# Three dense stages of a decoder kernel divided into parts, with gathered expert rows served between the parts

## The chip, the cores and the metric

The kernel runs on one core of a Trainium2 chip. The core has engines that run their own instruction streams and meet through semaphores: TensorE (PE, matmuls and transposes into PSUM), VectorE (DVE), ScalarE (ACT), GpSimd (POOL) and SyncE (SP), and 16 DMA engines. The metric is the device time of one execution in microseconds. The kernel before took 3770.63 us as the median of three runs, which lie between 3755.8 and 3774.13.

## The reference

Two layers over 512 tokens of width 1024. Each layer computes three branches from one projection of the normed input, adds them through gates, then adds a mixture over 16384 single-neuron experts (PEER), then a small gated embedding.

```python
h = _rms(x, g_mix)
z = h @ w_in                       # diff q,k,v | mla latents | conv B,C,value | 3 gates
y_d = _diff_attention(dq, dk, dv, ...)          # 4 heads of 2 x 64, QK-norm, ALiBi
y_m = _mla(cq, ckv, kr, g_cq, w_uq, g_ckv, w_ukv, g_q, g_k)
y_c = _short_conv(cb, cc, cx, conv_w)
mixed = g0 * (y_d @ w_br_diff) + g1 * (y_m @ w_br_mla) + g2 * (y_c @ w_br_conv)
x = x + mixed @ w_out
x = x + _peer(_rms(x, g_ffn), w_query, sub_keys, u_experts, v_experts)
x = x + sigmoid(_rms(x, g_ple) @ w_ple_gate) * (p_i @ w_ple_proj)

# inside _mla
q  = (_rms(c_q, g_cq) @ w_uq)      # 512 x 256 @ 256 x 768, 8 heads of 96
kv = (_rms(c_kv, g_ckv) @ w_ukv)   # 512 x 128 @ 128 x 1024, 8 heads of 64 (k) + 64 (v)
# q and k: RMSNorm over the 96 of a head, then RoPE on the last 32, then causal attention

# inside _peer, for each token: 8 heads choose 16 experts each, 128 rows of two tables
act = gelu(einsum('thkd,td->thk', u_tab[expert], hc))
out = einsum('thk,thkd->td', gate * act, v_tab[expert])
```

## The kernel before, in words

All data is f32. The tokens are worked in halves of 256 of one layer; a half is called d, from 0 to 3 (d = 0 and 1 are layer 0, d = 2 and 3 layer 1), and consists of two token tiles of 128. The program goes in steps from -1 to 4. In step s the dense stages of half s + 1 run (projections, both attentions, convolution, gates, output, and the choice of the experts), and beside them the expert rows of half s.

An *expert row* is, for the 128 tokens of a token tile, one chosen expert per token: one indirect DMA by POOL brings 128 x 2048 floats (1 MB: a row of u and a row of v) into one of 8 slots of `ring`. A half has 256 such rows (128 per token tile). DVE multiplies the u part with the token and sums (line 1173, a *dot*); ACT takes the gelu (line 750) and multiplies with the gate (line 752, the *weight*). Then the v part is added in one of two ways, fixed ahead by `BY_PE`: either DVE multiplies with the weight and adds to x (line 1182), or ACT makes a diagonal matrix of the weights (line 758, four of them in turn) and PE adds diag times v in `ps_sum` (line 1299, two matmuls of 512 columns, which the profile records as four). POOL may issue the gather of row n only when row n - 8 is added, so a slot that PE or DVE does not finish holds back all later gathers.

The order is a plan that all engines follow. `stages_of(step)` lists the stages, and `ROWS_IN` says how many expert rows go in front of each; `timeline()` turns this into a whole number of rows. On each engine the program then is `serve(rows)`, stage, `serve(rows)`, stage. For DVE and ACT `serve` does the rows at once. PE keeps the rows of a stage in a list `fresh` and does them behind the stage, when the next stage's `serve` comes, unless a slot or a diagonal is needed sooner: for most stages the next `serve` does them before that stage's own matmuls; for stages in `ROWS_LAST` (the scores among them) behind the stage. In step -1 and step 4 no rows are served.

PSUM has three banks that PE fills for ACT (`ps_act`) and three for DVE (`ps_dve`), each used in turn: PE may begin the fourth when the first is emptied (an evacuation, line 523 on ACT).

The stages that the change touches, for each half:
- `diff_turn`: after the q and k of the differential attention are normed on DVE, PE transposes them (line 1345), 4 heads x (q, k) = 8 banks of 256 columns, and ACT empties each into `diff_qT` or the key cache, with a gain.
- `mla_up`, called *up* here: PE multiplies the normed latents with `w_uq` (line 1495) and `w_ukv` (line 1498): per token tile four banks, which ACT empties in six activations (the two banks of k and v in two pieces each). Then DVE sums the squares for the norms (`mla_sums`, line 951 first), norms and turns.
- `mla_turn`, called *mla's turn*: PE transposes the finished q and k of 8 heads, 16 banks, ACT empties each (96 x 256). The scores of the first head (line 1430, 1432) wait for the last of them. DVE takes the scores (line 1020), ACT takes the exponential (line 537).

## Time and profile before

| | |
|---|---|
| median of three runs | 3770.63 us (3755.8 to 3774.13) |
| profiled execution, its own time | 3764.78 us |
| its span | 3762.9 us |
| mean granted PE clock | 0.893 of full |
| busy share PE, DVE, ACT, POOL | 78%, 66%, 40%, 35% |
| bytes moved by DMA | 1298.53 MB, mean 345 GB/s |
| gathers of expert rows | 1024, median 11.8 us from issue to landing |

The profile is one execution. In its rows a time in square brackets is how long the engine sat idle before the group, with the engine that released it. Matmuls in f32 appear as two records each, so one expert row on PE is x4. PEclk is the clock that was granted to PE as a share of full speed. The gathers begin at about 490 us, and from about 3120 us on only the last expert rows run, beside nothing dense; between them lie steps 0, 1 and 2.

### The profile page before, as it was taken

The numbers are of one execution on the slowest core, as the hardware profiler recorded it, in microseconds if no ns is written. First come the engines' busy times: TensorE is split into PE (matmuls) and PEld (weight loads), VectorE is DVE, ScalarE is ACT, GpSimd is POOL, SyncE is SP. The second block draws the span as 40 slices with busy tenths as digits, with TensorE's granted clock in tenths as the row PEclk, the third lists the DMA queues.
The fourth block names the chain that finished last, engine by engine and source line by source line (L and its number), as shares of the span: only waits on it lengthen the run. The fifth ranks groups of instructions, "written<-read, shape, count | busy, mean of one in ns | idle before, by whom it ended". The sixth has DMA issues, their size and how long they took to land.

```text
span 3762.9 us, 28794 instructions
## 1 busy us (share of the span) xinstructions
PE 2923.3 (78%) x8144; PEld 1489.6 (40%) x8144; DVE 2488.2 (66%) x5163; ACT 1486.5 (40%) x3998; POOL 1333.3 (35%) x1033
## 2 busy tenths in 40 slices
PE   7699858767988788767989788867998785555556
PEld 4454624534436334433436234524446331111112
DVE  1311487775667876876658877766657877777774
ACT  2230234467433344457432344458433342222222
POOL 0000043333332443344333443334333445555551
PEclk9889979988999899989999899889999997777778
DMA  4214379989998999989998999989999999999994
GB/s 151 81 67 162 121 319 384 378 337 343 393 385 348 394 402 386 395 351 407 405 377 322 409 410 381 357 340 361 382 389 360 390 405 419 422 422 422 422 421 185
DMA packets 182399, 1298.53 MB, mean 345 GB/s; under 512 B 20320, under 2 KB 21856, under 8 KB 26592
## 3 DMA queue, kind: packets, MB, share of 16 engines
q0 software_dynamic: 147456, 1073.81, 70.7%
q1 hardware_dynamic: 34784, 222.88, 15.1%
q8 instruction: 66, 1.08, 0.1%
q14 instruction: 93, 0.76, 0.1%
HBM read 1294.51 MB, written 2.10 MB: 345 GB/s over the span
## 4 chain that ended last, share of the span: by engine, by line
PE 47%; DMA 20%; DVE 14%; ACT 13%; issue 5%; POOL 1%; SPq 0%; DVEq 0%; ACTq 0%; POOLq 0%
DMA ring<-in_uv,experts 17%; PE ps_sum L1299 12%; PE ps_act L1361 8%; PE ps_act L1533 8%; PE ps_act L1406 7%; DVE ring L1173 5%; DMA wt<-in_weights 4%; PE ps_dve L1361 3%; DVE x L1182 2%; PE ps_dve L1561 2%; ACT L750 2%; ACT L537 2%; ACT diag L758 2%; ACT weight L752 2%; ACT area_e L537 2%
## 5 line engine op out<-in xcount | busy, mean ns | idle before, releaser
L507 POOL DMA_INDIRECT ring<-in_uv,experts x1024 | 1330.8, 1300 | 2358.3 <-DVE x L1182 915.6
L1299 PE MATMUL ps_sum<-ring,diag 128*128 128x512 f32 x2120 | 1228.6, 723 | 660.1 <-ACT diag L758 654.1
L1173 DVE SCALAR_TENSOR_TENSOR ring<-ring,h_ffn 128x1024 f32<-128x1024 f32 x1024 | 1233.4, 1219 | 207.3 <-DMA ring<-in_uv,experts 201.2
L1299 PEld LDWEIGHTS ps_sum<-ring,diag 128*128 128x128 f32 x2120 | 440.1, 222 | 1328.9 <-ACT diag L758 921.6
L1182 DVE SCALAR_TENSOR_TENSOR x<-ring,weight,x 128x1024 f32<-128x1024 f32 x494 | 633.0, 1281 | 220.0 <-ACT weight L752 219.9
L750 ACT ACTIVATE dots<-dots 128x1 f32<-128x1 f32 x1024 | 205.5, 201 | 1350.7 <-DVE ring L1173 1348.2
L1406 PE MATMUL ps_act<-area_h,wt 128*128 128x256 f32 x1536 | 345.1, 383 | 2.6 <-ACT area_h L523 2.6
L1533 PE MATMUL ps_act<-wt,area_h 128*128 128x512 f32 x768 | 339.5, 597 | 9.2 <-DMA wt<-in_weights 9.1
L1361 PE MATMUL ps_act<-wt,area_h 128*128 128x512 f32 (+1 forms) x768 | 332.5, 593 | 5.1 <-ACT area_h L523 5.1
L1406 PEld LDWEIGHTS ps_act<-area_h,wt 128*128 128x128 f32 x1536 | 293.1, 192 | 58.1 <-issue 15.3
L752 ACT ACTIVATE weight<-dots,gate 128x1 f32<-128x1 f32 x1024 | 301.6, 295 | 33.3
L1533 PEld LDWEIGHTS ps_act<-wt,area_h 128*128 128x128 f32 x768 | 145.2, 191 | 197.3 <-issue 177.1
L1361 PEld LDWEIGHTS ps_act<-wt,area_h 128*128 128x128 f32 x768 | 149.3, 196 | 182.9 <-issue 175.0
L523 ACT ACTIVATE area_b<-ps_act 128x256 f32<-128x256 f32 (+1 forms) x208 | 87.8, 437 | 335.0 <-PE ps_act L1406 143.7
L758 ACT ACTIVATE diag<-ident,weight 128x128 f32<-128x128 f32 x530 | 212.9, 402 | 17.4
L750 ACT ACT_TABLE_LOAD x143 | 183.5, 1283 | 2.5
L1561 PE MATMUL ps_dve<-wt,area_t 128*128 128x512 f32 x384 | 168.7, 592 | 0.0
L1345 PE MATMUL ps_act<-ident,area_b 128*128 128x128 f32 (+1 forms) x448 | 84.9, 336 | 87.2 <-DVE area_b L815 41.7
L537 ACT ACT_TABLE_LOAD x107 | 137.3, 1283 | 1.9
L1034 DVE TENSOR_TENSOR area_b<-ps_dve,area_b 128x512 f32<-128x512 f32 x32 | 22.1, 691 | 150.3 <-PE ps_dve L1561 150.3
L1020 DVE CUSTOM_DVE_ANT_0 area_e<-ps_dve,mask 128x128 f32<-128x128 f32 (+3 forms) x64 | 31.2, 489 | 124.1 <-PE ps_dve L1432 67.6
L1361 PE MATMUL ps_dve<-wt,area_b 128*128 128x512 f32 x256 | 110.9, 594 | 1.9 <-ACT area_b L523 1.9
(171 smaller groups left out, 2107.1 us busy)
## 6 DMA issues: line engine op xcount, KB each, us to landing
wt<-in_weights SPq DMA_DIRECT2D x192, 1024.0 KB, 8.9
ring<-in_uv,experts POOLq DMA_INDIRECT x1024, 11.8
wt<-in_weights SPq DMA_DIRECT2D x12, 512.0 KB, 8.9
wt<-in_weights SPq DMA_DIRECT2D x4, 768.0 KB, 8.9
x<-in_x SPq DMA_DIRECT2D x4, 512.0 KB, 5.2
area_y<-in_keys SPq DMA_DIRECT2D x4, 512.0 KB, 9.8
area_f<-in_keys SPq DMA_DIRECT2D x4, 512.0 KB, 11.2
area_f<-in_ffn_rows SPq DMA_DIRECT2D x4, 512.0 KB, 4.5
```

The lines of the kernel that those rows point to most:

```text
L507: pool.indirect_dma_start(ring[:, row.slot, :], None, a[f"uv{row.step // 2}"][:, :], bass.IndirectOffsetOnAxis(ap=experts[:, row.step % 2, ...
L537: act.activation(*args, **kw).then_inc(act_ops, 1)
L750: act.activation(dots[:, j], dots[:, j], ACT.Gelu).then_inc(gelu_ready, 1)
L752: act.activation(weight[:, j], dots[:, j], ACT.Copy, scale=gate[:, row.step % 2, row.tile, j])\
L758: act.activation(diag[:, row.pe_before % DIAGS, :], ident[:, :], ACT.Copy, scale=weight[:, j])\
L1173: dve.scalar_tensor_tensor(u, u, 1.0, h_ffn[:, row.tile, :], ALU.mult, ALU.mult, accum_out=dots[:, row.j:row.j + 1]).then_inc(dots_ready, 1)
L1182: dve.scalar_tensor_tensor(xs, ring[:, row.slot, D:2 * D], weight[:, row.j:row.j + 1], xs, ALU.mult, ALU.add)\
L1299: ins = pe.matmul(ps_sum[:, b, :], diag[:, row.pe_before % DIAGS, :], ring[:, row.slot, D + b * 512:D + (b + 1) * 512], start=row.pe_first ...
L1361: ins = pe.matmul(banks[t][:, 0:width], lhsT[:, 4 * kh + k, t * P:(t + 1) * P], w[:, k, 0:width], start=(kh + k == 0), stop=(kh == 1 and k ...
L1406: ins = pe.matmul(b[:, 0:HALF], w[:, k, c * P:(c + 1) * P], hT[:, k, :], start=(k == 0), stop=(k == KT - 1))
L1533: ins = pe.matmul(bank, hT[:, 4 * kh + k, t * P:(t + 1) * P], w[:, k, :], start=(kh + k == 0), stop=(kh == 1 and k == 3))
L1561: ins = pe.matmul(b, (ydT, ymT, ycT)[br][:, k, t * P:(t + 1) * P], w[:, k, :], start=(k == 0), stop=(k == 3))
```

## The change

Three stages are listed in parts. `diff_turn` becomes two stages of two heads each, `mla_up` two stages of one token tile each, `mla_turn` four stages of two heads each. The number of rows in front of them is divided in the same way (1.5 into 2 x 0.75, 5 into 2 x 2.5, 4 into 4 x 1). The scores wait for the last part. The weight tiles of up are released after its second part, as before.

```diff
-    "diff_sq": (0, 0, 0, 2), "diff_norm": (0, 1, 0, 3), "diff_turn": (8, 0, 0, 0),
+    "diff_sq": (0, 0, 0, 2), "diff_norm": (0, 1, 0, 3), "diff_turn": (4, 0, 0, 0),
-    "mla_norm": (3, 5, 0, 5), "mla_up": (8, 4, 0, 0), ... "mla_turn": (16, 0, 0, 0),
+    "mla_norm": (3, 5, 0, 5), "mla_up": (4, 2, 0, 0), ... "mla_turn": (4, 0, 0, 0),
 ROWS_IN = {
-    ... "diff_turn": 1.5, ... "mla_up": 5, ... "mla_turn": 4, ...
+    ... "diff_turn": 0.75, ... "mla_up": 2.5, ... "mla_turn": 1, ...
@@ stages_of
-        out += [..., ("qkv", d, 2), ("diff_turn", d)]
+        out += [..., ("qkv", d, 2), ("diff_turn", d, 0), ("diff_turn", d, 1)]
-        out += [("mla_norm", d), ("mla_up", d), ("mla_sums", d), ("mla_qk", d), ("mla_rope", d), ("mla_turn", d)]
+        out += [("mla_norm", d), ("mla_up", d, 0), ("mla_up", d, 1), ("mla_sums", d), ("mla_qk", d), ("mla_rope", d)]
+        out += [("mla_turn", d, part) for part in range(4)]
@@ ACT
-            def diff_turn(at, d):
-                for h in range(DH):
+            def diff_turn(at, d, part):
+                for h in range(2 * part, 2 * part + 2):
-            def mla_up(at, d):
-                for t in range(2):
+            def mla_up(at, d, t):
-            def mla_turn(at, d):
-                for h in range(MH):
+            def mla_turn(at, d, part):
+                for h in range(2 * part, 2 * part + 2):
@@ PE
-                pe.wait_ge(evacs, WHERE[("diff_turn", d)].evacs + 8)
+                pe.wait_ge(evacs, WHERE[("diff_turn", d, 1)].evacs + 4)
-            def mla_up(at, d):
-                pe.wait_ge(evacs, at.evacs)
+            def mla_up(at, d, t):
+                if t == 0:
+                    pe.wait_ge(evacs, at.evacs)
...
-                release(2)
+                if t:
+                    release(2)
-                pe.wait_ge(evacs, WHERE[("mla_turn", d)].evacs + 16)
+                pe.wait_ge(evacs, WHERE[("mla_turn", d, 3)].evacs + 4)
```

The plan gives these rows in front of the stages: up 4, 5, 5 rows at d = 1, 2, 3, now 2 + 2, 3 + 2, 3 + 2; mla's turn 4 each, now 1 + 1 + 1 + 1; diff's turn 2 each, now 1 + 1. Which rows go by PE is unchanged, and so is the order on DVE.

On PE at d = 1, from the first matmul of up to the second head's scores, before (L1495 and L1498 are up, L1299 expert rows at two matmuls each, L1345 with 96x128 mla's turn, L1430 and L1432 the scores):

```order
L1495 MATMUL ps_act<-wt,area_f 128x512 x2
L1495 MATMUL ps_act<-wt,area_f 128x256 x2
L1498 MATMUL ps_act<-wt,area_f 128x512 x2
L1299 MATMUL ps_sum<-ring,diag 128x512 x20
L1345 MATMUL ps_act<-ident,area_b 96x128 x32
L1430 MATMUL ps_dve<-kept_mla_kT,area_b 128x256
L1432 MATMUL ps_dve<-area_kv,area_b 128x128
L1299 MATMUL ps_sum<-ring,diag 128x512 x6
```

And in the changed kernel, at the same place:

```order
L1299 MATMUL ps_sum<-ring,diag 128x512 x4
L1495 MATMUL ps_act<-wt,area_f 128x512 x2
L1495 MATMUL ps_act<-wt,area_f 128x256 x2
L1498 MATMUL ps_act<-wt,area_f 128x512 x2
L1299 MATMUL ps_sum<-ring,diag 128x512 x16
L1345 MATMUL ps_act<-ident,area_b 96x128 x8
L1299 MATMUL ps_sum<-ring,diag 128x512 x2
L1345 MATMUL ps_act<-ident,area_b 96x128 x8
L1299 MATMUL ps_sum<-ring,diag 128x512 x2
L1345 MATMUL ps_act<-ident,area_b 96x128 x16
L1430 MATMUL ps_dve<-kept_mla_kT,area_b 128x256
L1299 MATMUL ps_sum<-ring,diag 128x512 x2
```

The first half of up stands ahead of the first row shown. Two rows (x4) moved from behind up to between its halves, and two of the three rows that stood behind the first scores now stand between quarters of the turn, one each. At d = 3 the quarters hold rows at other places (16 transposes, a row, 8, a row, 8), and none stands behind the first scores.

On ACT at d = 3, from the diag of up's third expert row on, before (L523 is the evacuation, L750 gelu, L752 weight, L758 diag):

```order
L758 ACTIVATE diag<-ident,weight 128x128
L750 ACTIVATE dots<-dots 128x1
L752 ACTIVATE weight<-dots,gate 128x1
L758 ACTIVATE diag<-ident,weight 128x128
L750 ACTIVATE dots<-dots 128x1
L752 ACTIVATE weight<-dots,gate 128x1
L523 ACTIVATE area_b<-ps_act 128x512
L523 ACTIVATE area_b<-ps_act 128x256
L523 ACTIVATE area_b<-ps_act 128x4x64
L523 ACTIVATE area_kv<-ps_act 128x256
```

And in the changed kernel (where the evacuation's line is L524):

```order
L758 ACTIVATE diag<-ident,weight 128x128
L524 ACTIVATE area_b<-ps_act 128x512
L524 ACTIVATE area_b<-ps_act 128x256
L524 ACTIVATE area_b<-ps_act 128x4x64
L524 ACTIVATE area_kv<-ps_act 128x256
L524 ACTIVATE area_b<-ps_act 128x4x64
L524 ACTIVATE area_kv<-ps_act 128x256
L750 ACTIVATE dots<-dots 128x1
L752 ACTIVATE weight<-dots,gate 128x1
L758 ACTIVATE diag<-ident,weight 128x128
L750 ACTIVATE dots<-dots 128x1
L752 ACTIVATE weight<-dots,gate 128x1
```

The fourth and fifth expert row of up moved from ahead of its first evacuation to behind its sixth activation, between the two token tiles.

## Rows read from the trace of the kernel before

**Rows 1.** The page: its span, and busy us of the engines.
```profile
span 3762.9 us, 28794 instructions
...
PE 2923.3 (78%) x8144; PEld 1489.6 (40%) x8144; DVE 2488.2 (66%) x5163; ACT 1486.5 (40%) x3998; POOL 1333.3 (35%) x1033
```

**Rows 2.** Waits in 500:3000 (DVE) and 2470:2535 (POOL): total us, times, longest.
```profile
DVE ring L1173 <- DMA ring<-in_uv,experts: 39.8, 37, 12.1
...
POOL ring L507 <- PE ps_sum L1299: 31.0, 4, 16.1
```

**Rows 3.** Timeline, POOL and DVE, up at d = 3: start, us, what [idle before].
```profile
2486.22 0.94 POOL L507 DMA_INDIRECT ring<-in_uv,experts  x1 [16.07 <-PE ps_sum L1299]
...
2494.48 1.22 DVE L1173 SCALAR_TENSOR_TENSOR ring<-ring,h_ffn 128x1024 f32<-128x1024 f32 x1 [12.13 <-DMA ring<-in_uv,experts]
...
2496.82 1.75 DVE L951 TENSOR_TENSOR area_e<-area_b 128x1536 f32<-128x1536 f32 x1
```

**Rows 4.** Timeline, PE, up at d = 3.
```profile
2471.47 4.54 PE L1495 MATMUL ps_act<-wt,area_f 128*128 128x512 f32 x8 [0.86 <-ACT area_f L523]
...
2478.81 1.13 PE L1498 MATMUL ps_act<-wt,area_f 128*128 128x512 f32 x2 [1.94 <-ACT area_b L523]
2479.78 2.74 PE L1495 MATMUL ps_act<-wt,area_f 128*128 128x512 f32 x8
...
2484.07 8.75 PE L1299 MATMUL ps_sum<-ring,diag 128*128 128x512 f32 x20
```

**Rows 5.** Timeline, ACT, up at d = 3.
```profile
2474.56 0.40 ACT L758 ACTIVATE diag<-ident,weight 128x128 f32<-128x128 f32 x1
...
2478.18 1.12 ACT L523 ACTIVATE area_b<-ps_act 128x512 f32<-128x512 f32 x3
...
2486.76 0.29 ACT L752 ACTIVATE weight<-dots,gate 128x1 f32<-128x1 f32 x1
```

**Rows 6.** Timeline, DVE, up at d = 1.
```profile
785.22 1.28 DVE L1182 SCALAR_TENSOR_TENSOR x<-ring,weight,x 128x1024 f32<-128x1024 f32 x1 [4.32 <-ACT weight L752]
...
796.18 1.23 DVE L1173 SCALAR_TENSOR_TENSOR ring<-ring,h_ffn 128x1024 f32<-128x1024 f32 x1 [0.62 <-DMA ring<-in_uv,experts]
```

**Rows 7.** Timeline, DVE and PE, up at d = 2.
```profile
1634.61 1.28 DVE L1182 SCALAR_TENSOR_TENSOR x<-ring,weight,x 128x1024 f32<-128x1024 f32 x1 [5.71 <-ACT weight L752]
...
1625.80 2.07 PE L1498 MATMUL ps_act<-wt,area_f 128*128 128x512 f32 x2 [4.37 <-ACT area_b L523]
```

**Rows 8.** Timeline, ACT, PE and POOL, mla's turn at d = 1.
```profile
822.98 0.46 ACT L523 ACTIVATE area_b<-ps_act,mq_gain 96x256 f32<-96x256 f32 x1
...
828.86 0.48 ACT L523 ACTIVATE area_kv<-ps_act,cols 96x256 f32<-96x256 f32 x1
...
836.87 0.62 ACT L537 ACTIVATE area_e<-area_e,soft 128x384 f32<-128x384 f32 x1 [1.51 <-DVE soft L1020]
...
823.49 5.25 PE L1345 MATMUL ps_act<-ident,area_b 128*96 128x128 f32 x26 [6.28 <-ACT area_b L523]
...
830.16 5.32 PE L1299 MATMUL ps_sum<-ring,diag 128*128 128x512 f32 x12
...
832.31 0.94 POOL L507 DMA_INDIRECT ring<-in_uv,experts  x1 [11.72 <-PE ps_sum L1299]
```

**Rows 9.** Timeline, ACT, second exponential at d = 2 and d = 3.
```profile
1684.76 0.40 ACT L537 ACTIVATE area_e<-area_e,soft 128x128 f32<-128x128 f32 x1 [0.60 <-DVE soft L1020]
...
2542.57 0.62 ACT L537 ACTIVATE area_e<-area_e,soft 128x384 f32<-128x384 f32 x1
```

**Rows 10.** Windows over expert rows on PE: us, PE busy, PEclk, DMA share, GB/s.
```profile
627.20:630.90 3.70, 3.70 (x7) 0.50 0.88 363
783.10:793.40 10.30, 10.30 (x25) 1.00 0.88 352
```

**Rows 11.** Timeline, PE, rows behind diff's first scores, d = 2 and 3.
```profile
1479.80 3.78 PE L1299 MATMUL ps_sum<-ring,diag 128*128 128x512 f32 x4
...
2321.25 5.52 PE L1299 MATMUL ps_sum<-ring,diag 128*128 128x512 f32 x8
```

More of the change, by code:

```diff
@@ L127, in tiles_done @@
     if name == "mla_up":
-        return [("for_act", at.evacs + 8)] * 2
+        return [("for_act", at.evacs + 4)] * 2
     if name in ("conv_x", "branch_first", "branch_more"):
@@ L176, in stages_of @@
     if d < STEPS:
-        out += [("x_norm", d), ("qkv", d, 0), ("qkv", d, 1), ("diff_sq", d), ("diff_norm", d), ("qkv", d, 2), ("diff_turn", d)]
+        out += [("x_norm", d), ("qkv", d, 0), ("qkv", d, 1), ("diff_sq", d), ("diff_norm", d), ("qkv", d, 2), ("diff_turn", d, 0), ("diff_turn", d, 1)]
         out += attention("diff", d, DH, [("conv_c", d, 0), ("conv_c", d, 1), ("conv_x", d, 0), ("conv_x", d, 1),
@@ L212, in timeline @@
             base = [a + b for a, b in zip(base, counts(st))]
-            tiles = TILES_OF.get(st[0], 0)
+            tiles = TILES_OF.get(st[0], 0) if st[0] != "mla_up" or st[2] else 0
             if tiles:
@@ L647, in mla_norm @@
                 evac(ckvT, bank(HALF), scale=col("g_ckv", d // 2))
-            def mla_up(at, d):
-                for t in range(2):
-                    row = qm[:, t, :, :].rearrange("p h d -> p (h d)")
-                    evac(row[:, 0:512], bank())
-                    evac(row[:, 512:768], bank(256))
-                    for i in range(2):
-                        part = bank().rearrange("p (h d) -> p h d", h=4)
-                        evac(km[:, t, 4 * i:4 * i + 4, 0:MNOPE], part[:, :, 0:MNOPE], last=False)
-                        evac(mla_v[d % 2][:, t, 256 * i:256 * (i + 1)].rearrange("p (h d) -> p h d", h=4),
-                             part[:, :, MNOPE:MNOPE + MV])
+            def mla_up(at, d, t):
+                row = qm[:, t, :, :].rearrange("p h d -> p (h d)")
+                evac(row[:, 0:512], bank())
+                evac(row[:, 512:768], bank(256))
+                for i in range(2):
+                    part = bank().rearrange("p (h d) -> p h d", h=4)
+                    evac(km[:, t, 4 * i:4 * i + 4, 0:MNOPE], part[:, :, 0:MNOPE], last=False)
+                    evac(mla_v[d % 2][:, t, 256 * i:256 * (i + 1)].rearrange("p (h d) -> p h d", h=4),
+                         part[:, :, MNOPE:MNOPE + MV])
             def mla_qk(at, d):
@@ L1419, in nothing, with diff_turn @@
                 pass
-            def diff_turn(at, d):
+            def diff_turn(at, d, part):
                 pe.wait_ge(dve_ops, at.dve)
-                for h in range(DH):
+                for h in range(2 * part, 2 * part + 2):
                     for c in range(2):
@@ L1484, in mla_norm, with mla_turn @@
                     turn_tiles(lambda t: latent[:, t, k * P:(k + 1) * P])
-            def mla_up(at, d):
-                pe.wait_ge(evacs, at.evacs)
+            def mla_up(at, d, t):
+                if t == 0:
+                    pe.wait_ge(evacs, at.evacs)
                 uq = tile(0)[:, 0:1536].rearrange("p (k n) -> p k n", k=2)
                 ukv = tile(1)
-                for t in range(2):
-                    ts = slice(t * P, (t + 1) * P)
-                    for lo, hi in ((0, 512), (512, 768)):
-                        b = act_bank()
-                        for k in range(2):
-                            ins = pe.matmul(b[:, 0:hi - lo], cqT[:, k, ts], uq[:, k, lo:hi], start=(k == 0), stop=(k == 1))
-                        to_act(ins)
-                    for i in range(2):
-                        to_act(pe.matmul(act_bank(), ckvT[:, ts], ukv[:, 512 * i:512 * (i + 1)], start=True, stop=True))
-                release(2)
-            def mla_turn(at, d):
+                ts = slice(t * P, (t + 1) * P)
+                for lo, hi in ((0, 512), (512, 768)):
+                    b = act_bank()
+                    for k in range(2):
+                        ins = pe.matmul(b[:, 0:hi - lo], cqT[:, k, ts], uq[:, k, lo:hi], start=(k == 0), stop=(k == 1))
+                    to_act(ins)
+                for i in range(2):
+                    to_act(pe.matmul(act_bank(), ckvT[:, ts], ukv[:, 512 * i:512 * (i + 1)], start=True, stop=True))
+                if t:
+                    release(2)
+            def mla_turn(at, d, part):
                 pe.wait_ge(dve_ops, at.dve)
-                for h in range(MH):
+                for h in range(2 * part, 2 * part + 2):
                     for source in (qm, km):
```

6 lines of the change are left out of this document (3 added, 3 removed).

## The prediction

> **What bounds the kernel now.** I read the page first. Its busy shares [rows 1] name no engine at its limit: PE is busy 78% of the span and DVE 66%. Then I asked who waits for whom. Between 500 and 3000 us, where the expert rows run beside the dense layers, DVE waits for a gather 37 times and 39.8 us in all [rows 2], of 2500. So up to there it is not the transfers but the hand-over between PE, ACT and DVE that sets the pace. After that the last 240 rows stream alone, and nothing of the change lies there. The program works on four halves of 256 tokens (d = 0 to 3). For d = 0 no expert row runs beside the dense stages, so splitting a stage there puts nothing between its parts: cost 0. That leaves nine places: diff's turn, up and mla's turn, each at d = 1, 2 and 3. I looked at each in the timeline, engine by engine, and asked what ends last.
>
> One place stands out, up at d = 3. Of the 39.8 us above, 12.1 are one wait: POOL waited 16.07 us for PE to be done with a slot of the ring, issued the gather at 2486.22, and DVE got it at 2494.48 [rows 2, 3]. PE was busy with up from 2471.47 and came to the expert rows only at 2484.07, four records a row, 8.75 us for 20 records or 1.75 us a row [rows 4]. In the middle of up PE also waited 1.94 us for ACT, which served five expert rows first and began to empty banks at 2478.18 [rows 4, 5].
>
> **The change, part by part.** No arithmetic is added, and on DVE the order is what it was. The expert rows that stood ahead of a stage on ACT, or behind it on PE, now stand partly between its parts. So there is no new instruction to pay, only what each engine has in front of it. On PE, up gets two rows between its halves at each d, mla's turn two single rows between its quarters at each d, and diff's turn one row at d = 2 and d = 3 and none at d = 1. On ACT the gelu, weight and diag of the same rows are spread likewise.
>
> *Up at d = 3.* ACT serves three rows, the third done at 2474.96 [rows 5], and then empties the first bank, not at 2478.18. PE's fourth bank starts at about 2476.7 and the first half ends at about 2477.8 (the matmul of that bank now takes 1.13 us [rows 4]). The first expert row is done 1.75 us later, at 2479.5, and POOL issues at about 2480.0, 6.2 us sooner. The same transfer of 8.3 us (2486.22 to 2494.48) lands at 2488.3, and the sums, which now start 2.3 us behind it at 2496.82 [rows 3], start at 2490.6: -6.2. Another path could be later. PE's second half starts behind two rows, at 2481.3, takes 4.3 us as now (2479.78 to 2484.07 [rows 4]) and ends at 2485.6, 1.5 us later than now; the weight that DVE needs ahead of the sums comes at 2487.05 now, 3.0 us after PE's end [rows 5], then at 2488.6, and the sums could start at 2489.8. It is 0.8 us earlier than the transfer allows, so -7.0 is the most there is to win. With the PE clock at its lower level the two rows take 3.7 us each [rows 10], the second half ends at 2489.5, the weight comes at 2492.5 and the sums start at 2493.8: -3.0. I take -6.2, since PE has been busy for six microseconds there.
>
> *Up at d = 1.* Here DVE hardly waits for a gather (0.62 us). It waits 4.32 us for a weight, to 785.22 [rows 6], and ACT gives it right behind the last bank of up. Now PE puts two rows, 3.5 us, ahead of the second half. What PE wins back is the short stall in the middle and the gaps beside it, 0.8 us: the second half ends 2.7 us later, and so do the weight and the sums behind it. The wait of 0.62 us goes. Net +2.1; between 0, if ACT and not PE is what ends last, and +6 with two rows at 2.0 us more each.
>
> *Up at d = 2.* The same wait for a weight is 5.71 us, to 1634.61, but PE stood still for 4.37 us in the middle of up, since ACT had five rows to serve [rows 7]. ACT now starts 2.3 us sooner. 3.5 us of rows less this leaves a second half that ends 1.1 us later: +1.1, between 0 and +5.
>
> *Mla's turn.* At d = 1, ACT begins 16 evacuations at 822.98 and ends them 6.2 us later; PE has stood idle for 6.28 us by then. The first score follows, then three rows on PE in 5.32 us, the second score, and ACT waits 1.51 us for it [rows 8]. Split, the first four evacuations go as soon as the first row is served. But a quarter's fourth bank waits for ACT, then comes an expert row on PE, then the next quarter's transposes, and ACT waits for those. Going quarter by quarter with 1.75 us a row I get the last evacuation at 829.2, the same as now, and the second score 3.3 us earlier, of which ACT can use only the 1.51 it waited. With rows at the lower clock the last evacuation is 1.5 us later and the second score no earlier. At d = 2 ACT's wait is 0.60 us, at d = 3 it is none, since its chain of table loads and exponentials is full there [rows 9]. Rows at the full clock: -1.5, -0.5, 0; at the lower: 0, +0.9, +1.1. Both levels are there in the trace: 3.7 us for a row at a granted 0.50, 1.75 us at 1.00 [rows 10]. I take +0.5 for the three. The ends are -4.6 (12 of 16 evacuations out of the way at one d) and +5 (six rows of 3.7 us are 22, less three idle times of 6.3, plus the lower column's 2).
>
> On this the Trainium skill ("Perfetto Trace Analysis", Matmul Optimizations) speaks against the change: it wants matmuls to run back to back in batches, and three rows that ran together behind the first score are single now. By it the lower column, +2.0 for the three turns, would be the term. The two clock rows agree that a row can cost double.
>
> *Diff's turn.* At d = 1 only ACT's row moves, 0. At d = 2 and 3 one row goes from behind the first scores to ahead of them. It took 3.78 us at d = 2 and 2.76 at d = 3 (two rows in 5.52) [rows 11]. The second scores come after the same PE work as before; what is lost is that the first exponentials start later, at d = 2 by more than PE's row behind them hid. +0.7; between -3 (both rows at 1.75) and +3.8 (the row of d = 2 wholly in the way).
>
> **Sum.** -6.2 + 2.1 + 1.1 + 0.5 + 0.7 = -1.8 us. The low ends give -14.6, the high ends +16.8. The profiled execution took 3764.78 us (span 3762.9 [rows 1] and 1.9 around it), 5.9 below the median of the three runs, 3770.63. Against that median the forecast is 3769.
>
> The earlier gathers in the turn (at d = 1 POOL waits 11.72 us for PE [rows 8]) I count at nothing, since DVE's waits in the heads behind it are for PE and ACT. If they help, it is within the -4.6.
>
> **Rivals.** *A: the overlap is worth its face value.* Of 16 evacuations 12 are done before the last row is served, 12/16 of 6.2 = 4.6 us at each d, 14 together; up costs nothing at d = 1 and 2, and the whole 12.1 us go at d = 3. That is -26, or 3744.6. For it: PE's stalls of 1.94, 4.37 and 6.28 us behind ACT. Against: PE needs three free banks and has a row in each gap now, and in up at d = 3 the weight allows 7.0 at most. The skill ("Perfetto Trace Analysis", Optimizing Scalar/DVE Operations) says that where ACT causes bubbles elsewhere, smaller pieces may let work complete sooner. Chance 0.09.
>
> *B, slower: the inserted rows hold back the banks that ACT waits for.* Fourteen rows (six in up, six in mla's turn, two in diff's) at 3.7 us are 52 us; PE's idle times in the turns cover 19, and the gather at d = 3 still gives 6.2: +27, or 3797.6. It decides from the point where a moved row costs PE more than the idle time that it fills. For it: rows of 3.7 us are there. Against: PE has long been busy in the middle of up. Chance 0.07.
>
> *C: the gain is swallowed.* The 6.2 us of d = 3 are real, but a later wait takes them, a weight or a score, and the losses of d = 1 and 2 go the same way: 3770.6. For it: DVE's gaps are many and small. Against: no transfer paces these stretches, so a shift should stay. Chance 0.27. That the split does nothing at all is excluded by the instruction order.
>
> My own account has 0.57 and a range of its own from 3755 to 3785.
>
> **Numbers.** The three runs lie 0.5% apart (3755.8 to 3774.13), so less than 0.5%, 19 us, can't be told from no change. A is faster, B slower; C and my account are within, but for the last account's tails: faster 0.10, same 0.82, slower 0.08. The range of 3750 to 3785 holds C, nearly all of mine, and leaves out A and B.
>
> **What would show it.** In the profile after, at d = 3, DVE's wait for the gather ahead of the sums should be near 6 us in place of 12.1 and POOL's 16.07 near 10. At d = 1 DVE's wait for the weight in up should be moved, and the sums 2 us later counted from the first matmul of up. The 16 evacuations should be four groups over some 11 us that end where they end now, within 1.5 us, and three rows behind the first score should be one (d = 1, 2) or none (d = 3). I am wrong if the stretch from the first matmul of up to the second exponential differs by over 5 us at d = 1 or 2, or if the moved rows mostly run at the lower clock in up.

## The result, and the profile after

The changed kernel takes 3742.78 us (median of 4 runs, 3740.29 to 3744.64), the kernel before 3767.47 beside it: ratio 0.9943, 95% interval 0.9922 to 0.9963, or -21 us (the two medians alone would give 0.9934, -25 us, which is inside the interval; the ratios are used below). Measured twice more in later comparisons it gave 0.9953 (0.9939 to 0.9967) and 0.9952 (0.9936 to 0.9969), -18 us. Two executions far longer than all others (4225.14 us of the changed kernel, 5927.58 of the kernel with rows held) are in no ratio. The forecast was 3769 us with no difference to be told; it was wrong.

The page of the changed kernel, as in [rows 1]:

```profile
span 3739.5 us, 28814 instructions
...
PE 2918.6 (78%) x8144; PEld 1484.7 (40%) x8144; DVE 2488.8 (67%) x5163; ACT 1484.6 (40%) x3998; POOL 1338.3 (36%) x1033
```

The work is the same. The waits of 500 to 3000 us on DVE, and of up and mla's turn at d = 3 on POOL (total us, times, longest), as in [rows 2]:

```profile
DVE ring L1173 <- DMA ring<-in_uv,experts: 30.2, 42, 2.1
...
POOL ring L508 <- PE ps_sum L1299: 29.0, 9, 7.0
```

The 12.1 us wait for a gather is gone, but DVE's waits for gathers fell by only 9.6 us in all, from 39.8 to 30.2. The other gain must be elsewhere.

Up at d = 3, PE, POOL, then DVE, against [rows 3, 4]:

```profile
2460.16 2.85 PE L1495 MATMUL ps_act<-wt,area_f 128*128 128x512 f32 x8 [0.86 <-ACT area_f L524]
...
2465.15 3.60 PE L1299 MATMUL ps_sum<-ring,diag 128*128 128x512 f32 x8
2468.58 2.74 PE L1495 MATMUL ps_act<-wt,area_f 128*128 128x512 f32 x8
...
2467.30 1.05 POOL L508 DMA_INDIRECT ring<-in_uv,experts  x1 [6.99 <-PE ps_sum L1299]
...
2472.90 1.23 DVE L1173 SCALAR_TENSOR_TENSOR ring<-ring,h_ffn 128x1024 f32<-128x1024 f32 x1 [1.83 <-DMA ring<-in_uv,experts]
2475.90 1.28 DVE L1182 SCALAR_TENSOR_TENSOR x<-ring,weight,x 128x1024 f32<-128x1024 f32 x1 [1.77 <-ACT weight L752]
2477.10 1.75 DVE L951 TENSOR_TENSOR area_e<-area_b 128x1536 f32<-128x1536 f32 x1
```

Two rows (x8) stand between the halves, POOL issues behind the first, and what DVE waits for last is the weight, as the prediction's upper bound had it.

Diff's turn at d = 2, PE and DVE, against [rows 11]:

```profile
1472.95 1.88 PE L1299 MATMUL ps_sum<-ring,diag 128*128 128x512 f32 x4
1474.67 1.39 PE L1345 MATMUL ps_act<-ident,area_b 128*128 128x128 f32 x8
1476.71 0.71 PE L1430 MATMUL ps_dve<-kept_diff_kT,area_b 64*128 64x128 f32 x6 [0.65 <-ACT kept_diff_kT L524]
1477.72 0.48 PE L1430 MATMUL ps_dve<-kept_diff_kT,area_b 64*128 64x128 f32 x2 [0.30 <-DVE soft L898]
1478.13 3.36 PE L1299 MATMUL ps_sum<-ring,diag 128*128 128x512 f32 x4
...
1477.79 0.28 DVE L898 CUSTOM_DVE_ANT_0 area_e<-ps_dve,dist 128x128 f32<-128x128 f32 x1
1478.24 0.29 DVE L898 CUSTOM_DVE_ANT_0 area_e<-ps_dve,dist 128x128 f32<-128x128 f32 x1 [0.16 <-PE ps_dve L1430]
```

The row ahead of the scores took 1.88 us; behind them it was 3.78. In the kernel before, PE went from the first transpose to the first and second scores so:

```profile
1474.04 0.60 PE L1345 MATMUL ps_act<-ident,area_b 128*128 128x128 f32 x4
...
1479.07 0.80 PE L1430 MATMUL ps_dve<-kept_diff_kT,area_b 64*128 64x128 f32 x4 [0.65 <-ACT kept_diff_kT L523]
...
1483.51 0.80 PE L1430 MATMUL ps_dve<-kept_diff_kT,area_b 64*128 64x128 f32 x4
```

That is 5.03 us to the first scores and 4.44 from there to the second. In the changed kernel it is 6.10 and 1.01: the row delays the first scores by 1.07 us, less than its own 1.88, since PE stops less for banks. At d = 3 the first part goes from 5.64 to 6.09 us and the second from 7.04 to 2.78: of the two rows behind the first scores (5.52 us, in a stretch at a granted clock of 0.66) one is left, and it took 1.98 us at 1.00.

Mla's turn at d = 1, PE, ACT and DVE, against [rows 8]:

```profile
821.18 1.88 PE L1299 MATMUL ps_sum<-ring,diag 128*128 128x512 f32 x4
822.90 1.37 PE L1345 MATMUL ps_act<-ident,area_b 128*96 128x128 f32 x8
824.10 1.88 PE L1299 MATMUL ps_sum<-ring,diag 128*128 128x512 f32 x4
...
831.58 2.83 PE L1299 MATMUL ps_sum<-ring,diag 128*128 128x512 f32 x4
...
823.32 0.47 ACT L524 ACTIVATE area_b<-ps_act,mq_gain 96x256 f32<-96x256 f32 x1 [0.47 <-PE ps_act L1345]
...
829.62 0.47 ACT L524 ACTIVATE area_kv<-ps_act,cols 96x256 f32<-96x256 f32 x1
...
836.39 0.61 ACT L538 ACTIVATE area_e<-area_e,soft 128x384 f32<-128x384 f32 x1
...
831.93 0.56 DVE L1020 CUSTOM_DVE_ANT_0 area_e<-ps_dve,mask 128x384 f32<-128x384 f32 x1 [4.19 <-PE ps_dve L1432]
835.21 0.56 DVE L1020 CUSTOM_DVE_ANT_0 area_e<-ps_dve,mask 128x384 f32<-128x384 f32 x1 [1.56 <-PE ps_dve L1432]
```

ACT's second exponential no longer waits. Windows over these stretches of the changed kernel (diff d = 2, behind its scores, diff d = 3, mla d = 1; the columns are those of [rows 10], with the other engines between):

```profile
1470.00:1478.00 8.00, 5.89 (x30) 3.27 (x28) 1.92 (x6) 6.05 (x18) 2.10 (x2) 1.00 1.00 424
...
1478.10:1481.50 3.40, 3.40 (x6) 1.52 (x6) 2.59 (x6) 3.37 (x10) 0.00 (x0) 0.57 0.92 313
...
2305.00:2317.00 12.00, 10.19 (x51) 6.42 (x50) 3.10 (x11) 9.07 (x25) 1.87 (x2) 1.00 0.99 410
819.00:830.00 11.00, 7.78 (x37) 3.94 (x35) 7.56 (x12) 8.81 (x28) 5.55 (x5) 1.00 1.00 373
```

Up to the scores the granted clock is 1.00 in all three, the 2.4 GHz level. Behind mla's first scores it fell in this execution (the row of 2.83 us above); in the second and third execution of the changed kernel that row took 1.88. In the kernel before, the stretch behind the first scores of diff's turn had 0.50, the 1.2 GHz level, at d = 2:

```profile
1479.00:1484.00 5.00, 4.93 (x12) 2.17 (x12) 0.51 (x4) 2.97 (x9) 0.15 (x1) 0.50 0.51 210
```

It fell behind transposes with stops between them (0.89 in 1476.5 to 1479). It still falls now, but behind the second scores (0.57, the row of 3.36 us).

**How the runs were read.** Two traces also differ outside the stages, by up to 12.5 us here, so the stages are compared one by one. DVE's instruction order is the same in every kernel here, so all 1024 dots can be laid beside each other, and a stage has an interval that leaves out what happened before it. Three are used: *diff*, from the start of the last DVE operation of diff_norm (L884) to DVE's taking of the fourth pair of scores (L898); *up*, from the first instruction behind the normalisation (L938) to the sums (L951); *mla*, from the first instruction behind the last rotary addition (L1013) to the fourth score (L1020). In us, at d = 1, 2 and 3 each; the last column is the ratio's difference in us of 3762. In the names, "only diff" is the kernel with that stage alone divided, "held" means that PE keeps its rows behind the stage, "ahead" that PE does them in front of it; each is described below.

```
                     diff                 up                   mla                  ratio
before               47.95 47.15 48.56    17.17 21.09 27.22    28.35 26.73 26.38
before again         47.97 46.89 48.60    17.17 22.77 27.29    28.36 27.00 26.38     -1
changed              46.41 45.85 44.82    20.10 22.55 18.81    25.80 24.67 25.70    -21
changed, 2nd         46.53 45.57 45.53    18.69 22.57 19.92    25.52 24.67 25.09    -18
changed, 3rd         44.94 45.48 44.65    18.70 22.56 18.81    25.52 24.66 25.09    -18
only diff            46.41 45.40 44.87    17.16 22.37 28.98    28.45 26.94 26.85     -3
only up              43.59 47.18 48.21    20.04 20.86 18.82    28.58 26.81 26.79     -9
only mla             46.63 46.91 48.56    17.16 22.77 27.21    25.52 24.66 25.97     -6
diff, mla            47.44 45.74 44.65    17.16 22.35 27.34    25.73 24.67 25.92     -8
same, rows held      46.41 47.30 48.55    17.15 21.11 27.22    27.41 26.05 24.48     -3
up at d = 3 only     47.97 45.70 44.65    17.16 22.50 18.81    25.52 24.67 25.09    -18
whole, rows ahead    44.86 43.78 45.88    17.17 22.49 28.99    29.27 28.52 29.80     -7
held in mla d = 3    47.91 45.39 45.40    17.16 22.35 19.92    25.52 24.67 24.76    -16
finer parts          45.42 47.61 47.34    17.15 22.55 19.91    30.59 28.01 26.74     -5
up, rows held        46.42 47.36 49.95    16.68 17.42 24.72    28.52 26.80 26.77    -12
combination          44.85 44.77 45.88    16.68 19.12 18.82    25.52 24.80 25.08    -23
diff ahead           46.13 44.66 46.15    17.16 22.50 27.37    28.39 26.94 26.39     -6
up mixed             46.42 47.18 48.60    15.25 17.43 19.92    28.39 26.74 26.44    -14
```

What kernels that do not touch a stage show there is the noise of one execution: diff at d = 1 ran from 43.59 to 47.97 and tells nothing; up at d = 2 has two values, 21.1 and 22.4 to 22.8 when whole; the rest agree within 0.6, but for up at d = 3 (28.98 twice) and diff at d = 3 once (49.95).

### The profile page after: what moved, and what is told of

Its sections match the earlier page's. It is cut to its first block, busy times and chain, and to the rows that moved or that the text cites. A ratio compares the mean times of both kernels' runs of the same rounds, so it can differ in the third digit from the quotient of the medians.

```text
span 3739.5 us, 28814 instructions
## 1 busy us (share of the span) xinstructions
PE 2918.6 (78%) x8144; PEld 1484.7 (40%) x8144; DVE 2488.8 (67%) x5163; ACT 1484.6 (40%) x3998; POOL 1338.3 (36%) x1033
## 4 chain that ended last, share of the span: by engine, by line
PE 46%; DMA 19%; DVE 15%; ACT 13%; issue 5%; POOL 1%; SPq 0%; DVEq 0%; ACTq 0%; POOLq 0%
DMA ring<-in_uv,experts 16%; PE ps_sum L1299 12%; PE ps_act L1534 8%; PE ps_act L1361 8%; PE ps_act L1406 7%; DVE ring L1173 5%; DMA wt<-in_weights 4%; PE ps_dve L1361 3%; DVE x L1182 2%; PE ps_dve L1562 2%; ACT L750 2%; ACT L538 2%; ACT diag L758 2%; ACT weight L752 2%; ACT area_e L538 2%
## 5 line engine op out<-in xcount | busy, mean ns | idle before, releaser
L1299 PE MATMUL ps_sum<-ring,diag 128*128 128x512 f32 x2120 | 1235.9, 726 | 661.2 <-ACT diag L758 655.0
L1299 PEld LDWEIGHTS ps_sum<-ring,diag 128*128 128x128 f32 x2120 | 441.5, 223 | 1331.7 <-ACT diag L758 927.6
L750 ACT ACTIVATE dots<-dots 128x1 f32<-128x1 f32 x1024 | 205.4, 201 | 1330.2 <-DVE ring L1173 1327.8
L752 ACT ACTIVATE weight<-dots,gate 128x1 f32<-128x1 f32 x1024 | 301.6, 295 | 33.3
L524 ACT ACTIVATE area_b<-ps_act 128x256 f32<-128x256 f32 (+1 forms) x208 | 87.5, 437 | 340.6 <-PE ps_act L1406 140.2
L758 ACT ACTIVATE diag<-ident,weight 128x128 f32<-128x128 f32 x530 | 212.8, 402 | 17.4
L1345 PE MATMUL ps_act<-ident,area_b 128*128 128x128 f32 (+1 forms) x448 | 81.5, 318 | 71.8 <-DVE area_b L815 39.6
L1562 PEld LDWEIGHTS ps_dve<-wt,area_t 128*128 128x128 f32 x384 | 73.0, 190 | 91.8 <-issue 91.8
```

Source lines behind the costliest of these rows:

```text
L750: act.activation(dots[:, j], dots[:, j], ACT.Gelu).then_inc(gelu_ready, 1)
L752: act.activation(weight[:, j], dots[:, j], ACT.Copy, scale=gate[:, row.step % 2, row.tile, j])\
L758: act.activation(diag[:, row.pe_before % DIAGS, :], ident[:, :], ACT.Copy, scale=weight[:, j])\
L1299: ins = pe.matmul(ps_sum[:, b, :], diag[:, row.pe_before % DIAGS, :], ring[:, row.slot, D + b * 512:D + (b + 1) * 512], start=row.pe_first ...
L1562: ins = pe.matmul(b, (ydT, ymT, ycT)[br][:, k, t * P:(t + 1) * P], w[:, k, :], start=(k == 0), stop=(k == 3))
```

## The experiments

All but the copies are made from the changed kernel with the number of parts as a table, by stage and d = 0 to 3, so that a stage can be whole or divided. With everything whole, the instruction orders are those of the kernel before.

**One stage at a time, and the kernel before again.**

```diff
-PARTS = {"diff_turn": (2, 2, 2, 2), "mla_up": (2, 2, 2, 2), "mla_turn": (4, 4, 4, 4)}   # the changed kernel
+PARTS = {"diff_turn": (2, 2, 2, 2), "mla_up": (1, 1, 1, 1), "mla_turn": (1, 1, 1, 1)}   # only diff
+PARTS = {"diff_turn": (1, 1, 1, 1), "mla_up": (2, 2, 2, 2), "mla_turn": (1, 1, 1, 1)}   # only up
+PARTS = {"diff_turn": (1, 1, 1, 1), "mla_up": (1, 1, 1, 1), "mla_turn": (4, 4, 4, 4)}   # only mla
```

> Only diff's turn is divided (two parts); up and mla's turn are whole as before. Read off the two traces, the stretch of diff's turn ended 1.6, 1.3 and 2.4 us earlier in the changed kernel at d = 1, 2 and 3, so the theory that the moved expert row is cheap ahead of the scores (1.88 us at a granted clock of 1.00 instead of 2.76 to 3.78 behind them) expects -5 us, most of it at d = 2 and 3, where a row on PE moves. The prediction on record (a row costs PE the same on either side) expects +0.7. If the whole gain is a property of the kernel's length or of the run, this is 0 and the before row's gap at d = 1 is not there.

> Only up is divided by token tile; both turns are whole as before. The prediction on record expects +2.1, +1.1 and -6.2 us at d = 1, 2 and 3, so -3. The two traces showed +2.1, +1.2 and -8.4, so -5. If up's evacuations left the path at their face value at every d, -10 or less.

> Only mla's turn is divided (four parts); up and diff's turn are whole as before. The prediction on record expects +0.5 us. The theory of the cheap moved row expects what the two traces showed, -3.9, -2.1 and -0.5 at d = 1, 2 and 3, so -6.5. The rival that this turn only gave back what up's division had delayed at d = 1 and 2 (+2.1 and +1.2 there) expects -6.5 + 3.3, so about -3 when up is whole.

> The kernel before, with nothing changed, as a second program. Of the changed kernel's 23.3 us, 6.5 lie in stretches that the change does not touch. If these are what two executions of one program differ by, this trace differs from the trace of before by some us in the same stretches (about 582, 1000 to 1400, 1900 to 2200 us and behind mla's turn at d = 3), in either direction, and the ratio's interval holds 1. If they come from the change, this trace agrees with the trace of before within 1 us there.

Measured, five rounds: only diff 0.9993 (0.9981 to 1.0005), only up 0.9975 (0.9961 to 0.9988), only mla 0.9984 (0.9972 to 0.9996), before again 0.9997 (0.9984 to 1.001). In us that is -3, -9 and -6 (each uncertain by 5), together the -18 of the changed kernel. The intervals of each stage change with that stage alone, up to the noise named. "Only diff" shortens diff's turn at d = 3 by 3.7 us and is then 1.7 us later at the sums of up. The division is not the cause of that: "diff, mla" has the same division and 27.34 there, and "whole, rows ahead", with nothing divided, has 28.99 (the last section has the record that goes with it). The ratio of "only diff" alone can't be told from 1. What the nine intervals leave of the difference in span is of the execution: -7.5 us for the changed kernel, as much for before again, and between -12.5 and +7.7 for the others.

**Rows held back on TensorE.** Both turns divided, up whole; ScalarE's order as when divided, TensorE's as before, since its late rows are not done ahead of any part but the first.

```diff
-                if name not in TICKS and name not in ROWS_LAST:
+                if name not in TICKS and name not in ROWS_LAST and not part:
                     add_rows(late, len(late))
```

> Diff's turn in two parts and mla's turn in four, up whole. By the runs with one turn divided at a time (-2.6 and -6.0 us by their ratios) the two together give -8.6. Both theories expect this; it is the partner of the next kernel.

> The same division, but TensorE does no expert rows between the parts: it keeps them behind the first scores, and its order is that of the kernel before, instruction for instruction. Only ScalarE's evacuations stand divided, with their rows in front of each part. Theory 1 (the gain is the price of the moved rows on TensorE, 1.88 us ahead of the scores against 2.76 to 3.78 behind them, and the second scores that come earlier for it) expects the gain gone: 0, with second scores where they were before. Theory 2 (the gain is ScalarE's: the evacuations are done earlier, so that the second exponential starts without an idle stretch) expects the gain kept, -8.6. Between the two: -2 to -6, both have a share.

> The changed kernel again, beside the kernels that it is to be compared with. Its ratio on record is 0.9943, -21 us. The three parts alone gave -2.6, -9.4 and -6.0, so -18.0 if they add up; more than -18 by 4 us or less would be theirs to explain together, and the intervals of 4 to 5 us each can hold that.

0.9980 (0.9969 to 0.9992) with the rows between the parts, 0.9992 (0.9983 to 1.0002) with the rows held. The interval of diff goes back to before at d = 2 and 3 (47.30, 48.55). On PE of the held kernel, diff d = 2 and mla d = 1:

```profile
1485.95 3.78 PE L1311 MATMUL ps_sum<-ring,diag 128*128 128x512 f32 x4
...
827.47 6.25 PE L1311 MATMUL ps_sum<-ring,diag 128*128 128x512 f32 x12
```

The two ratios overlap; the intervals tell the kernels apart. At diff's turn theory 1 holds and ScalarE's division is worth nothing. At mla's turn both have a share: held, 0.9, 0.7 to 1.0 and 1.9 us are won, and with the rows between 2.6 to 2.8, 2.1 to 2.3 and 0.4 to 1.3. Held, the last evacuation ended 10.6 us behind the rotary addition at d = 1, where it was 13.1 before, but the rows behind the first scores took 6.25 us where they had taken 5.32, and ACT then waited 2.84 us for the second score. At d = 3 the fourth score was earlier in the held order (24.48) than in any execution with the rows between (25.09 at best).

**Up divided at d = 3 alone.**

```diff
+PARTS = {"diff_turn": (2, 2, 2, 2), "mla_up": (1, 1, 1, 2), "mla_turn": (4, 4, 4, 4)}
```

> The changed kernel with up whole at d = 0, 1 and 2 and divided at d = 3 alone. If up's division costs 2.1 and 1.2 us at d = 1 and 2, as both traces and the prediction have it, this is 3.3 us faster than the changed kernel (-24 against the kernel before). If mla's turn takes that back anyway (it showed -3.9 and -2.1 behind a divided up, but -2.5 and about -1.3 behind a whole one), the difference is 1 us or less, which five rounds can't tell from none.

0.9952 (0.9939 to 0.9964) beside 0.9953 for the changed kernel in the same comparison. The sums at d = 1 are 1.5 to 2.9 us earlier (17.16), at d = 2 the same. The difference is too small for the ratio, and no gain is shown.

**Whole stages, TensorE's rows ahead.**

```diff
-              "mla_qk", "mla_rope", "mix_turn", "rank", "topk")
+              "mla_qk", "mla_rope", "diff_turn", "mla_turn", "mix_turn", "rank", "topk")
```

> Nothing is divided. TensorE does the expert rows that were served in front of diff's and of mla's turn ahead of the whole turn, not behind its first scores; ScalarE's and VectorE's orders are those of the kernel before. If the position of the row on TensorE is all of the gain at diff's turn (the runs with that turn divided put the fourth score 1.5 us earlier at d = 2 and 3.7 at d = 3, and the run that held the rows back gave none of it), diff's turn gains here as much as when divided: 1.5 and 3.7. At mla's turn TensorE has to wait for ScalarE's three weights first, so the transposes start some 6 us later and the evacuations behind them: the first score is then up to 5 us later and the second about as before. Sum by this: -5 for diff's turns and 0 to +9 for mla's, so -5 to +4, with the fourth scores to be read off. If a row needs the division to be cheap, diff's turn gains nothing and the sum is 0 or above.

0.9982 (0.9968 to 0.9996). Without any division, diff's fourth scores come at 43.78 and 45.88, at d = 2 at least as early as when divided (45.4 to 45.9), at d = 3 0.4 to 1.2 us later (44.7 to 45.5). At mla's turn PE waits for ScalarE's weights first, as expected, and loses 0.9, 1.5 to 1.8 and 3.4 us there. The nine intervals add up to +0.1 us against before and -1.7 against before again; the ratio says -7, uncertain by 5, at the edge of agreeing.

**Rows held at mla's turn at d = 3 alone; finer parts; up with its rows held.** The second kernel has these parts; the third holds the rows back as above, with up alone divided.

```diff
+ serve(name, units, name == "mla_turn" and d == 3 and more[0])      # first: held there only
+PARTS = {"diff_turn": (4, 4, 4, 4), "mla_up": (1, 1, 1, 2), "mla_turn": (8, 8, 8, 8)}
```

> Diff's turn in two and mla's turn in four, up divided at d = 3 alone, and in mla's turn at d = 3 TensorE keeps its rows behind the first scores (the order of before there). Counted from the last rotary addition, the fourth score of mla's turn at d = 3 started at 26.4 us in the kernel before, at 25.1 to 26.0 with rows between the parts and at 24.5 with the rows held back. So 0.6 to 1.5 us less than the run with up divided at d = 3 alone (0.9952): about 0.9949. If the order at d = 3 does not matter, the same 0.9952. Five rounds can't tell these two by the ratio; the fourth score in the trace can.

> As the run with up divided at d = 3 alone (0.9952), but diff's turn in four parts of one head and mla's in eight. Five rows are served in mla's turn's front, so finer parts put at most one row in front of a part as now, and the last row still comes late. If ScalarE's overlap is what is left to gain (first score 12.5 us behind the last rotary addition), it comes 0.5 us earlier at each d, -1.5 in all. If the first score is already bound by VectorE's dots, which the rows' weights wait for, 0. If each part adds a stop of TensorE behind a row (0.5 to 0.95 us, as ScalarE's waits between the quarters show), slower by 1 to 3 us.

> Only up is divided, and TensorE keeps its two rows behind the whole stage, in the order of the kernel before; only ScalarE's rows and evacuations are interleaved. With the rows between the halves the two traces had +2.0 us at d = 1 and -8.3 at d = 3. If the cost at d = 1 is the two rows on TensorE (3.6 us in front of the second half), it is gone here, 0. If the gain at d = 3 is the slot of the ring that a row between the halves frees earlier (POOL waited 16.07 us for it, 6.99 in the changed kernel), it is gone too: 0 to -2, and the sum is 0 to -2. If the gain at d = 3 is ScalarE's (the first bank emptied before the third to fifth row's weights), it stays: -6 to -8.

The first gave 0.9957 (0.9942 to 0.9971), its fourth score at 24.76: 0.33 us ahead of the order it replaces in "up at d = 3 only", and no gain is shown by the ratio. Finer parts gave 0.9986 (0.9975 to 0.9997) and 3757.42 us, 11 us more than the first kernel's 3745.97 beside it, and worse than the dearest case expected. The fourth scores of diff's turn too are later than with two parts (47.61 and 47.34 at d = 2 and 3). ACT at mla's turn, d = 1:

```profile
814.71 0.47 ACT L535 ACTIVATE area_b<-ps_act,mq_gain 96x256 f32<-96x256 f32 x1 [1.57 <-PE ps_act L1357]
...
818.68 0.47 ACT L535 ACTIVATE area_b<-ps_act,mq_gain 96x256 f32<-96x256 f32 x1 [1.57 <-PE ps_act L1357]
...
826.17 0.47 ACT L535 ACTIVATE area_b<-ps_act,mq_gain 96x256 f32<-96x256 f32 x1 [3.23 <-PE ps_act L1357]
```

And PE, the first and the last of the three rows between the parts:

```profile
812.47 1.98 PE L1311 MATMUL ps_sum<-ring,diag 128*128 128x512 f32 x4 [1.56 <-ACT diag L770]
...
822.28 3.64 PE L1311 MATMUL ps_sum<-ring,diag 128*128 128x512 f32 x4 [0.79 <-ACT diag L770]
```

A part of one head is two banks. PE's row waits for the diagonal that ACT makes behind the part before; ACT has emptied the next two banks before PE is done with that row, and waits for the row in turn. The last of these rows took 3.64 us.

Up with its rows held gave 0.9969 (0.9956 to 0.9982), where 0 to -2 us, or -6 to -8, were expected. At d = 1 the cost is gone (16.68), and at d = 2 the sums are 3.7 to 5.3 us earlier than before, which no theory had. PE there:

```profile
1620.03 1.13 PE L1511 MATMUL ps_act<-wt,area_f 128*128 128x512 f32 x2 [2.08 <-ACT area_b L535]
1621.00 2.74 PE L1508 MATMUL ps_act<-wt,area_f 128*128 128x512 f32 x8
1623.58 1.88 PE L1511 MATMUL ps_act<-wt,area_f 128*128 128x512 f32 x4
```

In the kernel before it waited 4.37 us and took 2.07 for the first of these [rows 7]. The shorter stop is ScalarE's division, and in this run the second half's eight matmuls behind it took 2.74 us (3.22 in the kernel before). At d = 3, 2.5 us stay of the 8.4; POOL:

```profile
2473.69 0.93 POOL L519 DMA_INDIRECT ring<-in_uv,experts  x1 [13.86 <-PE ps_sum L1311]
```

The other 5.9 need the row between the halves, which frees the slot; POOL waited 6.99 us with it.

**What was still open, and the combination.** Diff whole with its rows ahead ("diff_turn" alone added to ROWS_FIRST); up divided, with the row between the halves at d = 3 alone; both with mla's turn in four.

```diff
+ serve(name, units, name == "mla_up" and d < 3 and more[0])         # rows held at d = 1 and 2
```

> Nothing is divided; TensorE does diff's turn's row or rows ahead of the turn and not behind the first scores. All else is the kernel before. If diff's gain is the row's position alone, the fourth score of diff's turn is 3.1, 3.3 and 2.7 us earlier, as in the run that also moved mla's rows, and the sum is -5 to -9 us. If it needed the earlier mla's turn's order beside it, or if it is waited for again in up at d = 3 (where the run with diff alone divided had its sums 1.7 us later), -2 to -4 or nothing.

> Only up divided, and TensorE's rows stand between the halves at d = 3 alone, behind both at d = 1 and 2. Counted from the end of the normalisation on VectorE, the sums started 17.2, 21.1 to 22.8 and 27.2 us later in the kernel before, 20.0, 20.9 and 18.8 with the rows between, 16.7, 17.4 and 24.7 with the rows behind. Each half its own: 16.7, 17.4 and 18.8, so -0.5, -3.7 and -8.4, and -12.6 us together (0.9966). If the row between the halves at d = 1 and 2 was not the cause of the loss there, 20.0 and 20.9 stay.

> Diff's turn whole with its TensorE rows ahead of it; up divided, with TensorE's rows behind both halves at d = 1 and 2 and between them at d = 3; mla's turn in four as changed. By the intervals within the stages: diff's turns -3.1, -3.3 and -2.7 (fourth score), up -0.5, -3.7 and -8.3 (the sums), mla's turns -2.8, -2.2 and -0.9 (fourth score): -27.5 us together, 0.9927. If diff's and mla's gains don't add to up's (what is gained in front of a stage is waited for in it), it stays at the changed kernel's 0.995.

> The changed kernel again, as the measure for the combination: 0.9943 to 0.9953, as before.

Diff ahead gave 0.9985 (0.9971 to 0.9999). Its PE rows at d = 2:

```profile
1473.34 1.98 PE L1311 MATMUL ps_sum<-ring,diag 128*128 128x512 f32 x4 [1.54 <-ACT diag L770]
1475.16 2.85 PE L1357 MATMUL ps_act<-ident,area_b 128*128 128x128 f32 x16
```

PE waits 1.54 us for ACT's diagonal, and the fourth scores still come 2.2 to 2.5 us earlier at d = 2 and 3: at d = 2 diff's gain needs no division, and at d = 3 most of it does not. Up mixed gave 0.9963 (0.9948 to 0.9979), each half its own: 15.25, 17.43, 19.92. The combination gave 0.9940 (0.9925 to 0.9956) and 3740.33 us, beside 0.9952 and 3744.14 for the changed kernel. That is short of the -27.5 expected. It is the lowest median of all, but 4 us between two ratios that are each uncertain by 6 do not show that it beats the changed kernel.

## Why the prediction was wrong

In us at the end of a stage, changed less before, from the intervals, beside the terms (where before and before again differ, against both):

```
term           predicted       measured (three executions of the changed kernel)
up, d = 3      -6.2            -8.4, -7.3, -8.4
up, d = 1      +2.1            +2.9, +1.5, +1.5
up, d = 2      +1.1            -0.2 from 22.8, or +1.5 from 21.1
mla's turns    +0.5            -5.3 to -6.5 (d = 1: -2.6 to -2.8; 2: -2.1 to -2.3; 3: -0.7 to -1.3)
diff's turns   +0.7            -4.4 to -5.6 (d = 2: -1.0 to -1.7; 3: -3.0 to -4.0)
```

**The step that failed** at diff's turn is the price of the moved row: the prediction let it cost PE the same on either side of the scores. It ran in 1.88 us ahead of them, where it had taken 3.78 behind (d = 2), and delayed the first scores by less than that, 1.07 us, since it filled PE's stops. The bound "-3 (both rows at 1.75)" knew the price, but not the stops, nor at d = 3 that the row left behind would also be cheaper (1.98 us, where two took 5.52). Held back, diff's row cost 3.78 again and the gain was 0; moved ahead of an undivided turn, the gain at d = 2 was all there and at d = 3 most of it. This is shown.

**At mla's turns** two steps failed. The smaller is the weighing of two clock levels: +0.5 was taken, where the prediction's own column for rows at the full clock adds up to -2.0, and in the changed kernel every row moved into a turn ran in 1.88 to 2.21 us. That is 2.5 of the 5.8 to 7.0 us missed. The larger is the path: "the last evacuation at 829.2, the same as now". Counted from the rotary addition it ended 13.1 us on before and 11.8 with only this turn divided. So ACT could use more than the 1.51 us that it had waited, since the first exponential came 1.3 us sooner too, together the 2.8 measured at d = 1. The price of the rows was not what changed here: before, the three behind the first scores had run in 5.32 us, 1.77 each. Of the -5.3 to -6.5 the held run gives 3.5 to 3.8 to ScalarE's overlap, though its rows behind the scores were slower than before, so the shares are rough; and at d = 3 the two don't add: the held order alone won 1.9 there, the moved rows took up to 1.5 of it back. The Trainium skill ("Perfetto Trace Analysis", Optimizing Scalar/DVE Operations) says that breaking up instructions may let work complete sooner where ScalarE causes bubbles on other engines. Here the sequence of evacuations was broken up and no instruction; the overlap of the held run goes the same way, down to a size: eight parts lost 2.2 us at d = 1 where four had won 2.8. The Trainium skill ("Perfetto Trace Analysis", Matmul Optimizations) wants matmuls back to back in batches, and I applied that to the rows, which became single. In the trace the moved rows filled PE's stops: at mla's turn at d = 1 the granted clock was 1.00 from 819 to 830 us, where before it had been 0.69 in PE's idle time of 6.28 us and 0.50 in the first transposes behind it. So the page's rule did not speak against this change.

**Up** had the right mechanism. At d = 3 the last wait is the weight (1.77 us) as the -7.0 bound said. The size was 1.4 over that in two executions, and these are the ones where the first eight matmuls of up took 2.85 us; with 4.54, as in the kernel before, it is -7.3:

```profile
2453.31 4.54 PE L1495 MATMUL ps_act<-wt,area_f 128*128 128x512 f32 x8 [0.86 <-ACT area_f L524]
```

(the second execution of the changed kernel). At d = 1 the sign is right, the size between 1.5 and 2.9 by the same 4.4 or 2.85 us record. At d = 2 the +1.2 read off the first two traces (+1.5 by the interval), which seemed to bear out +1.1, does not hold against before again, whose up at d = 2 is 1.7 us longer. The divided up has two values there as well: 20.86 in "only up", where the two moved rows took 3.60 us together, and 22.55 to 22.57 in the changed kernel, where they took 5.17 to 5.29. Lower against lower and higher against higher the change is -0.2; that they belong together so is not shown.

**Rivals and signs.** A had the total (3744.6), but by luck: there are no 4.6 us of overlap at each d, and up's cost at d = 1 is real. Against A stood "PE has a row in each gap": true, and cheap. B is out, since no row moved into a turn cost 3.7, and the two of up at d = 2 took 5.2 and not 7.4. C is out too: the ratios show 18 to 21 us, and no later wait took them. Of the signs, POOL's wait was 6.99 (announced near 10) and the gather wait at the sums 1.83 (near 6), with the sums held by the weight. The sign for being wrong that should have caught it, 5 us from the first matmul of up to the second exponential, stayed silent: in the first two traces that stretch differs by only -0.4 us at d = 1 and -0.9 at d = 2, since at d = 1 up's loss and the gain of mla's turn nearly cancel in it, and diff's turn lies outside it. The sum missed some 6 to 7 us in the mla term, 5 to 6 in diff's and 3 to 4 in up's, about 16 in all, and they all had one sign. Those of mla and diff share a cause: moved work stood where its engine had been idle, or ended an idle time sooner, and was priced as if it did not. The range of 19 us below the forecast treated them as if they would offset each other.

## What to carry to other kernels

Work that one engine does in the gap of another has no price of its own: ask in which gap it will stand. Among transposes that wait for banks, a row of 1.88 us delayed diff's first scores by 1.07; behind the first scores at d = 2 it had cost its full 3.78 us, at a granted clock of 0.50. Behind mla's first scores the clock was 1.00 before the change, and the gain there came mostly from evacuations that ended sooner: the same division paid in two stages for two reasons. Before an interval of a stage is believed to a microsecond, look at it in executions that left that stage alone: one copy of the kernel before would have shown that up at d = 2 has two values.

## What the runs showed of the hardware

The same eight matmuls at the start of up at d = 3 took 2.85 us in some executions and 4.54 in others of one program, with the same wait of 0.86 us ahead; the divided up followed with its sums by 1.1 us. The granted clock over them was 1.00 in the one (2460.2 to 2462.8) and 0.59 in the other (2453.4 to 2457.6). The fast start is not always the good one: with up whole PE then stopped for 3.64 us instead of 1.94, the second half's eight then took 4.41 to 4.44 us instead of 2.74, and the sums came 1.7 us later (28.98 against 27.2). At d = 1 both starts of the whole up, 2.85 us with a stop of 1.81 and 4.33 with a stop of 0.34, ended alike, at 17.16. At d = 2, after a stop of 4.37 us, the second half's eight took 3.22 to 3.23 or 4.48 to 4.89, which are the two values there; with the rows held and a stop of 2.08 us they took 2.74 in two executions and 4.44 in a third.
